# Router logits with tokens as the moving operand in two halves, row squares shared with VectorE, and expert rows scaled and turned in halves

## The chip, the cores and the metric

One Trainium2 chip, one core. The metric is the device time of one execution in microseconds (us), lower is better. All data are fp32 except a few one-hot tables in fp16.

## The reference, cut to what matters

One inference step of a hybrid decoder layer: 512 prompt tokens and 8 sample tokens, 520 in all, of width 2048. The part around the change is the end of the mixer and the hierarchical mixture of experts:

```python
x = x + mix @ w_out                       # 2048 x 2048
h = rmsnorm(x, g_ffn_norm)
lg = h @ w_rg + b_rg                      # 4 expert groups
le = h @ w_re + b_re                      # 8 experts in each: 36 router columns in all
grp = argmax(lg)                          # top 1 of 4 groups, then top 2 of 8 in it
out = sum over 2 chosen e of gate_e * (silu(h @ w_g[e]) * (h @ w_u[e])) @ w_d[e]
y = rmsnorm(x + out, g_final)
```

w_g and w_u of one expert are 2048 x 512, w_d is 512 x 2048. There are 32 experts, 12 MB of weights each.

## The kernel before, in words

Everything is in one SBUF arena of named regions and one PSUM tile of 8 banks (512 fp32 each). Each engine has one instruction stream written by hand; the order between engines is set by semaphores (`wait_ge`, `then_inc`), and a wait holds all that stands behind it in its stream.

**Output projection and router.** PE computes the 16 column tiles of `mix @ w_out` in turn (`outproj`, matmuls issued on L533: 128x128 weights, two halves of 260 tokens, 16 contraction steps). VectorE adds each to the residual (L1403), which gives `x2`, with features on partitions. After tiles 4, 8 and 12, and after the last, PE runs `rows_of_x2(g)` for the four tiles of group g (0 to 3). It turns the x2 columns into rows by PE transposes (L727), for five token tiles (four of 128, one of 8), through three rotating PSUM banks; ScalarE copies each turned tile to SBUF (L976), which frees the bank, and squares it with a row sum (L980). Then PE adds the group's share to the router logits (L732): the tokens are the stationary operand (128x128 loads), the 36 router columns the moving one, 5 token tiles x 4 contraction steps. So logits end with tokens on partitions, in bank 7. SyncE stores the rows of each group to a DRAM table `x2_rows` and loads weights in between.

**Routing.** After group 3, VectorE sums the squares (L1407), ScalarE takes the root (L982), VectorE inverts it, puts it beside the rows (L1415, L1416; SyncE then stores group 3, with the scale, and issues three of the first expert's weight chunks behind it), scales the logits (L1419), and runs a long chain of small operations: maxima, one-hots, ranks (PE, L768), places in blocks. Two one-hot tables (L1497, L1500) are multiplied on PE (L774) and give, for each block of up to 64 tokens (CAP) of one expert, the list of its tokens. Lists become indices (L1505 to L1509). GpSimd gathers a block's 64 rows from `x2_rows` by an indirect DMA (`gather`, L1117).

**Blocks.** A block is: ScalarE scales its rows (L994, 64x2048) into `xsc`; PE turns them (`turn_rows`, L787, 16 transposes in two groups of 8); VectorE evacuates the two groups (L1523) into `xtr`; PE multiplies gate and up weights (L807; outputs of two column halves go to PSUM partitions 0 to 63 and 64 to 127), turns the activation (L813), multiplies the down weights (L823); ScalarE evacuates (L1008), GpSimd scatters the rows (L1128). PE turns the rows of block n+1 between the up and the down product of block n. There are 34 blocks in this run: one for each expert, and two more. SyncE loads each weight chunk (six of 2 MB per expert) when PE has released the same chunk of the expert before (`s_fr`, L458, L461). The first expert's chunks are loaded without such a wait.

What the change touches: `rows_of_x2` and its ScalarE and VectorE partners (L971 to L980, L1400 to L1420), the lists product (L773, L1497), `scale_rows` (L989), `turn_rows` (L778), the first waits of the PE `expert` (L797) and the GpSimd stream before the first gather (L1133).

```python
            for b in range(20):                      # ScalarE
                g, i = b // 5, b % 5
                act.wait_ge(s_tr, b + 1)
                A(part, ps[0:n, 4 + b % 3, :], ACT.Copy).then_inc(s_trev, 1)
                ...
                A(rowjunk[0:n], part, ACT.Square, accum_out=row_part[0:n, i, g:g + 1]).then_inc(s_rss, 1)
```

## Time and profile before

| | before |
|---|---|
| median of 3 runs | 2068.12 us (2067.97 to 2071.73) |
| the profiled execution's own time | 2068.49 us |
| its span in the trace | 2066.7 us |
| PE busy | 1762.6 us (85%) |
| VectorE, ScalarE, GpSimd busy | 509.8, 325.3, 287.2 us |
| HBM read | 517.52 MB, 265 GB/s over the span |
| granted TensorE clock, mean | 0.944 of full speed |

The span is the stretch from the first to the last instruction of that execution; its own time is the span and 1.8 us around it. The profile names for each group of instructions its line, its engine, its shape and its mean length. The chain of waits follows the execution back from its end, at each step to what released it. The stages on the clock of the trace: projections, state space and attention until about 675 us, the output projection and its router groups until 926 us, routing until 956 us, the expert blocks until about 2001 us, the final sum and norm until the end. A fp32 matmul leaves two records in the trace, a transpose one.

### The profile page before, as it was taken

The page shows a single profiled execution, that of the slowest core. Times are in us where ns is not written, and L with a number is a line of the kernel's source. Part 1 is how long each engine was busy: PE and PEld are TensorE (multiplying, and loading weights), DVE is VectorE, ACT ScalarE, POOL GpSimd, SP SyncE. Part 2 cuts the span into 40 slices and gives each one's busy share as a digit, 9 for nine tenths or more (in the row PEclk, how much of TensorE's full clock was granted, in tenths as well). Part 3 has the DMA queues.
Part 4 walks back from the last instruction along what each step waited for, and adds up shares of the span by engine and source line. Part 5 has one row for each costly group of instructions (what it writes and reads, how often), then busy time and mean ns, then how long its engine had stood idle before and what let it go on. Part 6 is the DMA issues. An engine that isn't in the chain of part 4 may idle for free.

```text
span 2066.7 us, 27101 instructions
## 1 busy us (share of the span) xinstructions
PE 1762.6 (85%) x10986; PEld 1238.5 (60%) x10987; DVE 509.8 (25%) x1090; ACT 325.3 (16%) x573; POOL 287.2 (14%) x225
## 2 busy tenths in 40 slices
PE   7999999999899999985887787778787888977880
PEld 6888888887578888873544444434444454544440
DVE  6410999535365200014000000000000000000006
ACT  4003111004623011111111110101010111101112
POOL 0681322215800000000000000000000000000000
PEclk9999999999999999997999999998999999999895
DMA  5264121336954223317999999999999597999995
GB/s 234 64 153 111 68 81 61 122 147 190 14 199 162 102 82 125 140 37 292 386 405 422 395 413 395 406 391 393 393 398 393 199 399 324 412 403 411 414 416 218
DMA packets 88821, 535.86 MB, mean 259 GB/s; under 512 B 28761, under 2 KB 37465, under 8 KB 43673
## 3 DMA queue, kind: packets, MB, share of 16 engines
q1 hardware_dynamic: 74528, 513.81, 66.0%
q0 software_dynamic: 8800, 19.17, 3.2%
q10 hardware_dynamic: 5440, 2.13, 0.6%
q8 instruction: 39, 0.64, 0.1%
q14 instruction: 14, 0.11, 0.0%
HBM read 517.52 MB, written 30.91 MB: 265 GB/s over the span
## 4 chain that ended last, share of the span: by engine, by line
PE 53%; DMA 38%; POOL 3%; DVE 3%; ACT 2%; issue 1%; SPq 0%; POOLq 0%; ACTq 0%; DVEq 0%
DMA arena<-w_up_in 36%; PE psum L533 35%; PE psum L807 11%; PE psum L823 2%; DMA arena<-y_rows 1%; PE psum L662 1%; PE psum L668 1%; PE psum L570 1%; PE psum L787 1%; DVE arena L1564 1%; PE psum L732 1%; DVE arena L1557 1%; DMA y_rows<-arena 0%; POOL arena L1040 0%; POOL arena L1043 0%
## 5 line engine op out<-in xcount | busy, mean ns | idle before, releaser
L533 PE MATMUL psum<-arena 128*128 128x260 f32 x3328 | 741.5, 386 | 18.0 <-ACT arena L845 13.1
L533 PEld LDWEIGHTS psum<-arena 128*128 128x128 f32 x3328 | 637.1, 192 | 118.5 <-issue 10.2
L807 PE MATMUL psum<-arena 128*64 128x256 f32 x4352 | 541.8, 408 | 177.3 <-DMA arena<-w_up_in 150.5
L807 PEld LDWEIGHTS psum<-arena 128*64 128x64 f32 x4352 | 331.3, 148 | 397.0 <-DMA arena<-w_up_in 174.2
L823 PE MATMUL psum<-arena 128*64 128x512 f32 x1088 | 255.0, 623 | 16.9 <-ACT arena L1003 16.1
L1550 DVE TENSOR_TENSOR arena<-arena,psum 128x256 f32<-128x256 f32 x34 | 14.3, 421 | 959.9 <-PE psum L807 959.9
L823 PEld LDWEIGHTS psum<-arena 128*64 128x64 f32 x1088 | 78.1, 143 | 171.9 <-issue 143.5
L1128 POOL DMA_INDIRECT y_rows<-arena x34 | 33.9, 996 | 986.3 <-ACT arena L1008 941.2
L1003 ACT ACTIVATE arena<-psum 128x256 f32<-128x256 f32 x34 | 13.1, 384 | 509.2 <-PE psum L813 509.2
L787 PEld LDWEIGHTS psum<-arena 64*128 64x128 f32 x560 | 64.8, 203 | 22.1 <-issue 22.1
L1008 ACT ACTIVATE arena<-psum 128x512 f32<-128x512 f32 x68 | 36.9, 594 | 261.2 <-PE psum L823 261.2
L787 PE MATMUL psum<-arena 64*128 64x64 f32 x560 | 69.6, 276 | 8.8 <-ACT arena L994 8.8
L994 ACT ACTIVATE arena<-arena 64x2048 f32<-64x2048 f32 x35 | 69.8, 1995 | 19.7 <-DMA arena<-x_rows,arena 17.2
L1403 DVE TENSOR_TENSOR arena<-psum,arena 128x520 f32<-128x520 f32 x16 | 11.2, 700 | 223.4 <-PE psum L533 223.4
L1254 DVE TENSOR_TENSOR arena<-arena 128x64 f32<-128x64 f32 x128 | 45.3, 354 | 79.5 <-ACT arena L865 69.3
L1523 DVE TENSOR_TENSOR arena<-psum,arena 128x512 f32<-128x512 f32 x70 | 48.4, 692 | 29.8 <-PE psum L787 29.7
L883 ACT ACTIVATE arena<-psum 64x520 f32<-64x520 f32 x16 | 9.6, 601 | 263.9 <-PE psum L533 148.5
L1135 POOL MEMSET arena<- 128x4 f32 x2 | 0.1, 102 | 364.0 <-PE psum L732 364.0
L1259 DVE TENSOR_TENSOR arena<-arena 128x64 f32 x128 | 49.2, 385 | 4.4
L976 ACT ACTIVATE arena<-psum 128x512 f32<-128x512 f32 (+1 forms) x20 | 11.6, 581 | 225.4 <-PE psum L727 225.4
L1257 DVE TENSOR_TENSOR arena<-arena 128x64 f32<-128x64 f32 x128 | 46.4, 362 | 0.0
L1073 POOL TENSOR_TENSOR arena<-arena 128x520 f32<-128x520 f32 x16 | 20.8, 1300 | 170.5 <-ACT arena L885 131.8
(294 smaller groups left out, 1076.1 us busy)
## 6 DMA issues: line engine op xcount, KB each, us to landing
arena<-w_down_in SPq DMA_DIRECT2D x64, 2048.0 KB, 26.1
arena<-w_gate_in SPq DMA_DIRECT2D x64, 2048.0 KB, 28.1
arena<-w_up_in SPq DMA_DIRECT2D x64, 2048.0 KB, 27.7
arena<-w_in_in SPq DMA_DIRECT2D x32, 1024.0 KB, 4.8
arena<-w_out_in SPq DMA_DIRECT2D x16, 1024.0 KB, 4.8
arena<-k_cache_in SPq DMA_DIRECT2D x8, 1024.0 KB, 6.8
arena<-v_cache_in SPq DMA_DIRECT2D x8, 1024.0 KB, 4.8
arena<-y_rows SPq DMA_DIRECT2D x8, 1024.0 KB, 8.1
```

What stands on the lines that cost most here:

```text
L533: last = mm(pair(n)[:, h, :], w(kk), rhs(kk)[:, HALF * h:HALF * (h + 1)], start=(kk == begin), stop=(kk == kn - 1 and stop))
L787: last = pe.transpose(ps[:, 3 + g, CAP * m:CAP * (m + 1)], rows[:, 8 * g + m, :], ident[0:CAP, 0:CAP])
L807: last = mm(ps[64 * h:64 * h + 64, i // 2, 0:256], xtr[:, kk, :], w[:, kk, 256 * h:256 * (h + 1)], start=(kk == 0), stop=(kk == 15))
L823: last = mm(ps[64 * h:64 * h + 64, 5 + b, :], act_col[:, kk % 2, 64 * (kk // 2):64 * (kk // 2) + 64], wd[:, kk, 1024 * h + 512 * b:1024 * ...
L994: A(xsc[0:CAP], xrow[j][0:CAP, 0:DM], ACT.Copy, scale=xrow[j][0:CAP, DM:DM + 1]).then_inc(s_sc_x, 1)
L1008: A(yrow[:, 512 * b:512 * (b + 1)], ps[:, 5 + b, :], ACT.Copy).then_inc(s_yv, 1)
L1073: tt(rope_t[:, 0], rope_in[:, m % 2, 0], cosr, ALU.mult)
L1128: pool.indirect_dma_start(out=y_rows, out_offset=bass.IndirectOffsetOnAxis(ap=idx_now[:, 2 + j:3 + j], axis=0), in_=yrow, in_offset=None, ...
L1254: tt(scan_t[:, 0], column(it * 4 + s), lam_same, ALU.mult).then_inc(s_scan, 1)
L1257: tt(scan_t[:, 2], scan_t[:, 0], column(it * 4 + (s + 1)), ALU.add).then_inc(s_scan, 1)
L1259: tt(column(it * 4 + (s + 1)), scan_t[:, 2], scan_t[:, 1], ALU.add).then_inc(s_scan, 1)
L1523: tt(xtr[:, 8 * g:8 * g + 8, :], ps[:, 3 + g, :].rearrange("p (k n) -> p k n", n=CAP), gtab[:, 8 * g:8 * g + 8].unsqueeze(2).to_broadcast( ...
```

## The change

- In `rows_of_x2` the router weights (128x36) become the stationary operand and the tokens the moving one, in two parts of 256 and 264 tokens that go to PSUM partitions 0 to 35 and 64 to 99 of bank 7. This product stands after the first three token tiles are turned and before the last two. After group 3 the 36x520 logits are copied to SBUF in two parts (ScalarE the second, between its copies of tiles 2 and 3; VectorE the first, before its square of tile 3), and PE turns them into token rows in bank 0 (five small transposes).
- The squares of group 3 move from ScalarE to VectorE. The two constant tables upper16 and ones16 are now made after the row scales instead of before the wait for the row sums.
- The slot one-hots are 64 columns wide instead of 128; PE writes the lists twice, to partitions 0 to 63 and 64 to 127, in 20 matmuls instead of 10.
- GpSimd issues an indirect DMA whose 64 indices are all out of bounds, once the logits are in PSUM, and waits for its end before it goes on to the first gather.
- `scale_rows`, and the waits in `turn_rows` and `expert`, go by halves: ScalarE scales the eight k of half g (64x1024, in runs of 8 elements), PE turns that half as soon as it is scaled, and the first two gate chunks wait for one half each.

```diff
--- before.py
+++ after.py
@@ -225,7 +225,8 @@
         s_rss, s_rrt, s_rrs = sem("row_sumsq"), sem("row_root"), sem("row_rstd")
         s_hr = sem("h_row_ready")
         s_x2st = sem("x2_stored")
-        s_lg = sem("logits_psum")
+        s_lg, s_lgc, s_lgr = sem("logits_psum"), sem("logits_copied"), sem("logit_rows_psum")
+        s_warm = sem("idle_transfer_done")
         s_ra, s_rb = sem("router_act"), sem("router_dve")
         s_pos = sem("positions_psum")
         s_hot, s_lst = sem("one_hots_ready"), sem("lists_psum")
@@ -267,6 +268,8 @@
         iota_b, iota_s, valid, tok, half_of = col(NBLK), col(P), col(5), col(5), col(1)
         router_const = view(ro_at + 642, NBLK + P + 11)
         logit = col(180).rearrange("p (t n) -> p t n", t=5)
+        cut = 2 * P
+        logit_cols = [region("X", cut, 520), region("X", T - cut, 520 + cut)]
 
         keep = Cols(ms + 4 * XW + DM // 2)
         gate_w = keep(10).rearrange("p (t j) -> p t j", t=5)
@@ -278,13 +281,14 @@
         more_i = keep(1).bitcast(U32)
+        idle_i = keep(1).bitcast(U32)
 
         rt = Cols(ea + 2 * XW)
-        lo16 = rt(5 * P).bitcast(F16).rearrange("p (c s) -> p c s", c=10)
+        lo16 = rt(5 * CAP).bitcast(F16).rearrange("p (c s) -> p c s", c=10)
         hv16 = rt(10 * NBLK).bitcast(F16).rearrange("p (c v b) -> p c v b", c=10, v=2)
         in_group, elow, rest, elow2, rank = (rt(160).rearrange("p (t e) -> p t e", t=5) for _ in range(5))
         hot = rt(320).rearrange("p (c e) -> p c e", e=NE)
@@ -716,24 +720,36 @@
 
             def rows_of_x2(g):
 
-                pe.wait_ge(s_x2, 4 * g + 4)
-                if g == 0:
-                    pe.wait_ge(s_gwr, 1)
-                for i, n in enumerate(TOKS):
-                    b = 5 * g + i
+                def turned_tile(i):
+                    n, b = TOKS[i], 5 * g + i
                     if b >= 3:
                         pe.wait_ge(s_trev, b - 2)
                     for m in range(4):
                         last = pe.transpose(ps[0:n, 4 + b % 3, P * m:P * (m + 1)],
                                             x2[:, 4 * g + m, P * i:P * i + n], ident)
                     last.then_inc(s_tr, 1)
-                for i, n in enumerate(TOKS):
-                    for kk in range(4 * g, 4 * g + 4):
-                        last = mm(ps[0:n, 7, 36 * i:36 * (i + 1)], x2[:, kk, P * i:P * i + n], wr[:, kk, :],
-                                  start=(kk == 0 and i == 0), stop=(kk == 15), skip_group_check=True)
+
+                pe.wait_ge(s_x2, 4 * g + 4)
+                if g == 0:
+                    pe.wait_ge(s_gwr, 1)
+                for i in range(3):
+                    turned_tile(i)
+                for kk in range(4 * g, 4 * g + 4):
+                    for h in range(2):
+                        last = mm(ps[64 * h:64 * h + 36, 7, 0:(cut, T - cut)[h]], wr[:, kk, :],
+                                  x2[:, kk, cut * h:(cut, T)[h]], start=(kk == 0), stop=(kk == 15),
+                                  skip_group_check=True)
                 if g == 3:
                     last.then_inc(s_lg, 1)
-
+                for i in range(3, 5):
+                    turned_tile(i)
+                if g == 3:
+                    pe.wait_ge(s_lgc, 2)
+                    for i, n in enumerate(TOKS):
+                        c = P * i - (cut if i >= 2 else 0)
+                        last = pe.transpose(ps[0:n, 0, 36 * i:36 * (i + 1)], logit_cols[i >= 2][0:36, c:c + n],
+                                            ident[0:36, 0:36])
+                    last.then_inc(s_lgr, 1)
 
             def outproj(n, k0, kn, begin=0, stop=True):
                 for kk in range(k0, kn):
@@ -771,18 +787,19 @@
 
             pe.wait_ge(s_hot, 1)
             for c in range(10):
-                last = mm(ps[:, 4, 0:2 * NBLK].rearrange("p (v b) -> p v b", v=2), lo16[:, c, :], hv16[:, c],
-                          start=(c == 0), stop=(c == 9))
+                for h in range(2):
+                    last = mm(ps[64 * h:64 * h + 64, 4, 0:2 * NBLK].rearrange("p (v b) -> p v b", v=2), lo16[:, c, :],
+                              hv16[:, c], start=(c == 0), stop=(c == 9), skip_group_check=True)
             last.then_inc(s_lst, 1)
 
             def turn_rows(n):
 
-                pe.wait_ge(s_sc_x, n + 1)
-                if not first(n):
-                    pe.wait_ge(s_xte, n * 2)
-                pe.sem_inc(s_turn, 1)
                 rows = xsc[0:CAP, :].rearrange("p (m k) -> p k m", k=16)
                 for g in range(2):
+                    pe.wait_ge(s_sc_x, n * 2 + (g + 1))
+                    if not first(n):
+                        pe.wait_ge(s_xte, n * 2 + (g - 1))
+                    pe.sem_inc(s_turn, 1)
                     for m in range(8):
                         last = pe.transpose(ps[:, 3 + g, CAP * m:CAP * (m + 1)], rows[:, 8 * g + m, :],
                                             ident[0:CAP, 0:CAP])
@@ -794,9 +811,10 @@
                 else:
                     pe.wait_ge(s_tab, 1)
                     loaded = pe.value_load(loads_i[0:1, bass.ds(n, 1)], min_val=16, max_val=16 * NE)
-                pe.wait_ge(s_xte, n * 2 + 2)
                 for i in range(4):
                     w, c = (wg, wu)[i // 2], i % 2
+                    if i < 2:
+                        pe.wait_ge(s_xte, n * 2 + (i + 1))
                     pe.wait_ge(s_ld[i], loaded)
                     if i == 0 and not first(n):
                         pe.wait_ge(s_si, n)
@@ -974,6 +992,11 @@
                 part = x2_of[i][0:n, 512 * g:512 * (g + 1)]
                 act.wait_ge(s_tr, b + 1)
                 A(part, ps[0:n, 4 + b % 3, :], ACT.Copy).then_inc(s_trev, 1)
+                if b == 17:
+                    act.wait_ge(s_lg, 1)
+                    A(logit_cols[1][0:36], ps[64:100, 7, 0:T - cut], ACT.Copy).then_inc(s_lgc, 1)
+                if g == 3:
+                    continue
                 act.wait_ge(s_trev, b + 1)
                 if b:
                     act.wait_ge(s_rss, b)
@@ -989,9 +1012,11 @@
             def scale_rows(n, j, it):
 
                 act.wait_ge(s_gat[j], it * 16 + 16)
-                if not first(n):
-                    act.wait_ge(s_xt, n * 2)
-                A(xsc[0:CAP], xrow[j][0:CAP, 0:DM], ACT.Copy, scale=xrow[j][0:CAP, DM:DM + 1]).then_inc(s_sc_x, 1)
+                for g in range(2):
+                    if not first(n):
+                        act.wait_ge(s_xt, n * 2 + (g - 1))
+                    part = [r[0:CAP, 0:DM].rearrange("p (m k) -> p m k", k=16)[:, :, 8 * g:8 * g + 8] for r in (xsc, xrow[j])]
+                    A(part[0], part[1], ACT.Copy, scale=xrow[j][0:CAP, DM:DM + 1]).then_inc(s_sc_x, 1)
 
             def expert(n, j, it):
                 scale_rows(n + 1, 1 - j, it + j)
@@ -1120,7 +1145,7 @@
                     bounds_check=T - 1, oob_is_err=False).then_inc(s_gat[j], 16)
 
             def expert(n, j, it):
-                pool.wait_ge(s_sc_x, n + 1)
+                pool.wait_ge(s_sc_x, n * 2 + 2)
                 gather(n + 2, j)
                 pool.wait_ge(s_is, n + 1)
                 pool.wait_ge(s_yv, n * 2 + 2)
@@ -1133,7 +1158,12 @@
             pool.wait_ge(s_lg, 1)
             for j in range(2):
                 pool.memset(xrow[j][:, DM:XW], 0.0).then_inc(s_z0, 1)
-            pool.wait_ge(s_z0, 2)
+            pool.wait_ge(s_z0, 3)
+            pool.indirect_dma_start(
+                out=xrow[0][0:CAP, 0:DM // 2], out_offset=None, in_=t["w_glu"].rearrange("a p n -> (a p) n"),
+                in_offset=bass.IndirectOffsetOnAxis(ap=idle_i[0:CAP], axis=0),
+                bounds_check=T - 1, oob_is_err=False).then_inc(s_warm, 16)
+            pool.wait_ge(s_warm, 16)
             pool.wait_ge(s_x2st, 16 * 8)
             for j in range(2):
                 gather(j, j)
@@ -1398,12 +1428,20 @@
                 stt(z2[:, n], z2[:, n], gso[:, n:n + 1], rz, ALU.mult, ALU.mult).then_inc(s_mix, 1)
 
             dve.wait_ge(s_x2l, 16)
+            dve.memset(idle_i, int(BIG) - 1).then_inc(s_z0, 1)
             for n in range(16):
                 dve.wait_ge(s_op, n + 1)
                 tt(halves(x2[:, n]), pair(n), halves(x2[:, n]), ALU.add).then_inc(s_x2, 1)
-            dve.tensor_copy(upper16, region("upper", P))
-            dve.memset(ones16, 1.0)
-            dve.wait_ge(s_rss, 20)
+            for i, n in enumerate(TOKS):
+                dve.wait_ge(s_trev, 16 + i)
+                if i == 0:
+                    dve.wait_ge(s_rss, 15)
+                if i == 3:
+                    dve.wait_ge(s_lg, 1)
+                    dve.tensor_copy(logit_cols[0][0:36], ps[0:36, 7, 0:cut]).then_inc(s_lgc, 1)
+                part = x2_of[i][0:n, 1536:DM]
+                stt(rowjunk[0:n], part, 1.0, part, ALU.mult, ALU.mult, accum_out=row_part[0:n, i, 3:4]).then_inc(s_rss, 1)
+                dve.wait_ge(s_rss, 16 + i)
             dve.tensor_reduce(row_sum, row_part, X, ALU.add).then_inc(s_rrs, 1)
             link(dve.memset(logit, 0.0))
             dve.wait_ge(s_rrt, 1)
@@ -1414,9 +1452,11 @@
             dve.memset(x2_of[4][:, DM + 1:XW], 0.0)
             dve.tensor_copy(x2row[:, :, DM:DM + 1], row_rstd[:, 0:4].unsqueeze(2))
             dve.tensor_copy(x2_of[4][:, DM:DM + 1], row_rstd[:, 4:5]).then_inc(s_hr, 1)
-            dve.wait_ge(s_lg, 1)
+            dve.tensor_copy(upper16, region("upper", P))
+            dve.memset(ones16, 1.0)
+            dve.wait_ge(s_lgr, 1)
             for i, n in enumerate(TOKS):
-                last = stt(logit[0:n, i, :], ps[0:n, 7, 36 * i:36 * (i + 1)], row_rstd[0:n, i:i + 1], rbias[0:n],
+                last = stt(logit[0:n, i, :], ps[0:n, 0, 36 * i:36 * (i + 1)], row_rstd[0:n, i:i + 1], rbias[0:n],
                            ALU.mult, ALU.add)
             link(last)
 
@@ -1494,7 +1534,7 @@
             tt(o_, o_, b_, ALU.add)
             link(stt(w_, b_, -float(CAP), p_, ALU.mult, ALU.add))
             link(stt(by_choice(w_), by_choice(w_), 1.0, both(valid), ALU.add, ALU.mult))
-            tt(lo16, iota_s.unsqueeze(1).to_broadcast([P, 10, P]), over(w_, P), ALU.is_equal)
+            tt(lo16, iota_s[:, 0:CAP].unsqueeze(1).to_broadcast([P, 10, CAP]), over(w_, CAP), ALU.is_equal)
             link(tt(wide_b, iota_b.unsqueeze(1).to_broadcast([P, 10, NBLK]), over(o_, NBLK), ALU.is_equal))
             tt(hv16[:, :, 0, :], wide_b, over(id_, NBLK), ALU.mult)
             tt(hv16[:, :, 1, :], wide_b, over(tok1, NBLK), ALU.mult).then_inc(s_hot, 1)
```

## Rows read from the trace of the kernel before

**Rows 1.** The page, its chain that ended last, by engine.
```profile
PE 53%; DMA 38%; POOL 3%; DVE 3%; ACT 2%; issue 1%; SPq 0%; POOLq 0%; ACTq 0%; DVEq 0%
```

**Rows 2.** Windows: PE, PEld, DVE, ACT, POOL busy (instructions), PE clock, DMA share, GB/s.
```profile
900.00:918.00 18.00, 17.91 (x82) 15.20 (x80) 0.75 (x2) 0.00 (x0) 0.00 (x0) 1.00 0.00 1
...
1100.00:1300.00 200.00, 160.31 (x1086) 85.67 (x1082) 11.77 (x30) 22.72 (x31) 11.70 (x12) 0.92 1.01 406
...
1600.00:1650.00 50.00, 40.76 (x296) 22.23 (x294) 1.92 (x5) 7.08 (x9) 3.90 (x4) 0.97 0.54 203
```

**Rows 3.** Timeline of router group 1: start, length, what, [idle before <- releaser].
```profile
802.14 1.95 PE L727 MATMUL psum<-arena 128*128 128x128 f32 x16
...
802.77 0.60 ACT L976 ACTIVATE arena<-psum 128x512 f32<-128x512 f32 x1 [58.52 <-PE psum L727]
...
804.03 0.58 ACT L976 ACTIVATE arena<-psum 128x512 f32<-128x512 f32 x1
...
804.67 0.60 PE L727 MATMUL psum<-arena 128*8 128x128 f32 x4 [0.58 <-ACT arena L976]
...
805.10 4.03 PE L732 MATMUL psum<-arena 128*128 128x36 f32 x40
```

**Rows 4.** Chain of waits: the projection behind router group 1 (start, length, what).
```profile
809.13 57.99 PE psum L533 x256
```

**Rows 5.** Chain of waits in a stretch of blocks that wait for no weights.
```profile
1640.69 13.81 PE psum L807 x128
1654.50 1.92 PE psum L787 x16
```

**Rows 6.** Timeline of router group 3 and the row sums.
```profile
917.95 0.70 DVE L1403 TENSOR_TENSOR arena<-psum,arena 128x520 f32<-128x520 f32 x1 [13.33 <-PE psum L533]
918.57 0.22 DVE L1404 CAST arena<-arena 128x128 f16<-128x128 f32 x1
...
918.71 2.01 PE L727 MATMUL psum<-arena 128*128 128x128 f32 x16 [0.79 <-DVE arena L1403]
918.76 0.17 DVE L1405 MEMSET arena<- 128x128 f16 x1
919.40 0.60 ACT L976 ACTIVATE arena<-psum 128x512 f32<-128x512 f32 x1 [45.51 <-PE psum L727]
...
925.73 0.17 DVE L1407 TENSOR_REDUCE arena<-arena 128x5 f32<-128x20 f32 x1 [6.80 <-ACT arena L980]
```

**Rows 7.** Timeline of the one-hots and the lists product.
```profile
939.85 1.49 DVE L1497 TENSOR_TENSOR arena<-arena 128x1280 f16<-128x1280 f32 x1
...
941.94 0.66 DVE L1499 TENSOR_TENSOR arena<-arena 128x480 f16<-128x480 f32 x1
...
943.23 0.98 PE L774 MATMUL psum<-arena 128*128 128x96 f16 x10 [8.15 <-DVE arena L1500]
```

**Rows 8.** Timeline of the first two gathers.
```profile
946.10 1.88 POOL L1117 DMA_INDIRECT arena<-x_rows,arena  x1 [20.03 <-DVE arena L1509]
...
948.29 0.95 POOL L1117 DMA_INDIRECT arena<-x_rows,arena  x1 [0.31 <-issue]
```

**Rows 9.** Chain of waits at the first gather.
```profile
946.10 4.75 DMA arena<-x_rows,arena
```

**Rows 10.** Windows beside the first gather (columns as in rows 2).
```profile
942.00:946.00 4.00, 0.98 (x10) 0.77 (x10) 2.82 (x9) 0.00 (x0) 0.00 (x0) 0.50 1.01 430
946.00:950.00 4.00, 0.00 (x0) 0.00 (x0) 3.19 (x5) 0.00 (x0) 2.84 (x2) 0.50 0.66 248
```

**Rows 11.** Timeline of the first block until its first released weight chunk.
```profile
950.88 2.00 ACT L994 ACTIVATE arena<-arena 64x2048 f32<-64x2048 f32 x1 [17.17 <-DMA arena<-x_rows,arena]
...
953.02 2.00 PE L787 MATMUL psum<-arena 64*128 64x64 f32 x16 [8.82 <-ACT arena L994]
954.25 1.50 DVE L1523 TENSOR_TENSOR arena<-psum,arena 128x512 f32<-128x512 f32 x2 [5.00 <-PE psum L787]
...
955.81 15.89 PE L807 MATMUL psum<-arena 128*64 128x256 f32 x128 [0.78 <-DVE arena L1523]
...
961.55 3.78 SPq L458 DMA_DIRECT2D arena<-w_gate_in  x2
```

**Rows 12.** Window in which the first block's PE clock rises (columns as in rows 2).
```profile
958.00:960.00 2.00, 2.00 (x14) 1.19 (x12) 0.20 (x2) 0.42 (x1) 0.94 (x1) 0.60 0.00 0
```

**Rows 13.** DMA to landing of all gathers (the line L1117), least, median, most.
```profile
DMA to landing us min/median/max: 3.6/13.7/16.8
```

**Rows 14.** Timeline: a later row scaling, in a block that waits for no weights.
```profile
1641.77 2.00 ACT L994 ACTIVATE arena<-arena 64x2048 f32<-64x2048 f32 x1
```

## The prediction

> **What bounds the kernel now.** I read the chain of waits first: PE holds 53% of it and DMA 38% [rows 1]. Two stages share the span between them, so I went on to windows [rows 2]. In the output projection (900 to 918 us) PE is busy 17.91 of 18 us at clock 1.00 and the DMA engines are idle: PE sets the time there, and whatever PE does between two column tiles adds to it. In the blocks (1100 to 1300) the DMA share is 1.01 at 406 GB/s while PE is busy only 160 of 200 us: there the stream of expert weights sets the time. The exception is around the two extra blocks (1600 to 1650, DMA share 0.54), where an expert has a second block and its weights can't be released; there PE sets the time for two or three blocks. Between the two stages, from 918 to 956 us, one chain of small steps runs through all engines. Its end matters: the second expert's first weight chunk is issued at 961.55 us, when PE has used the first block's first chunk, which began after 955.81 [rows 11]. From there the stream is full, so what is saved before 955.81 should arrive at the end whole, and what is changed inside the blocks should hardly show.
>
> **Router groups 0 to 2.** Group 1 stands for three alike. PE starts to turn at 802.14 [rows 3] and is back in the projection at 809.13 [rows 4]: 6.99 us. In it, 40 logit records take 4.03 us, some 0.10 each: the 128x128 loads set this pace. The fifth tile starts only at 804.67, when ScalarE's second copy is done (804.03 + 0.58).
> The new logits are 4 steps x 2 parts = 8 matmuls, 16 records, of 256 or 264 columns. The nearest row is the gate and up product: fp32, 256 columns, outputs alternating between partitions 0 to 63 and 64 to 127, 128 records in 13.81 us, 0.108 each [rows 5]. The projection, with 260 columns over all partitions, takes 57.99 / 256 = 0.227 each [rows 4]. So in the first form two run beside one another. I take 0.108, because the new outputs lie in the same two halves: 16 x 0.108 = 1.7 us. The other end is 16 x 0.227 = 3.6.
> Turning: 16 transposes in 1.95 us [rows 3], with the last one's own length in it, are 0.11 each. The new group is 12 x 0.11 = 1.35, logits 1.7, then 8 x 0.11 = 0.9: 4.0 us, and some 0.2 where forms change. ScalarE's second copy is over 2.5 us after the start (804.61 - 802.14), before the fifth tile comes up at 1.35 + 1.7 + 0.45 = 3.5, so this wait is gone and nothing takes its place; ScalarE's copies and squares run on beside the projection, which hides them. Saved: 7.0 - 4.2 = 2.8 us each, **8.4 us** for three. SyncE's stores wait for the row copies, which are not later than before, but for the last two tiles by about 1 us under 58 us of cover [rows 4].
> On the change of form the trace speaks where gate and up end and the turning begins: 13.81 us of L807 from 1640.69, and L787 starts in the chain at 1654.50, with no piece between [rows 5]; over 128 records at 0.108 that leaves no more than about 0.2 us for it. A group changes form twice, so the bounds are 0 and 0.4 us, and the 0.2 above is their middle. The Trainium skill ("TensorEngine Tiling (Array Packing)", Key Properties) says that a change of tiling mode drains TensorE, which speaks against a tiled product put between transposes. By it the upper bound would hold each time, 1.2 us over the three groups where the sum has 0.6; no row shows more.
>
> **Group 3 to the row scales.** Before, ScalarE copies and squares five tiles from 919.40, and the sum starts at 925.73 [rows 6]. Now ScalarE only copies, 0.60 each: tiles 0 to 2 are over at 921.2. PE turns three tiles by 920.1 and has the logits at 922.0. ScalarE takes its part of them (about 0.4), then copies tile 3 until 923.1 and tile 4 until 923.7. VectorE's squares are over SBUF, 512 elements; nearest is its 128x520 addition, 0.70 us [rows 6]. Squares 0 to 2 end at 922.3; square 3 waits for tile 3 at 923.1, then the logit copy (0.35), then squares 3 and 4: the last ends at 924.9. What is late next is thus the copy of tile 3, behind ScalarE's wait for the logits. **0.8 us** earlier than 925.73. The five small transposes wait for both copies and are over at about 924.2, under the root and the reciprocal. The two constant tables, once under cover at 918.57 and 918.76 (0.22 and 0.17 [rows 6]), now stand between the row scales and the logits: **0.3 us** lost.
>
> **Lists.** The one-hots shrink from 1280 to 640 elements. 1.49 us for 1280 and 0.66 for 480 [rows 7] give 1.04 ns per element: **0.7 us** saved. The product goes from 10 to 20 matmuls of 96 columns; 10 took 0.98. If pairs overlap as above, nothing changes; if not, it costs up to 0.8 more. I take 0.1 lost.
>
> **First gather.** Its issue took 1.88 us, the next one's 0.95 [rows 8]. The out-of-bounds transfer takes the first-time share earlier, in the 20.03 us in which GpSimd idles [rows 8]. I take **0.9 us**, off the 4.75 us from the start of its issue to its landing [rows 9]; the ends are 0 (the extra belongs to this table or to real rows) and 1.2 (the issue gap ahead of it shrinks too). Against it: the gather starts about 2 us sooner, while the first expert's chunks, issued behind the row store and so only 0.8 us sooner, may still be landing; DMA is full until 946, and 66% busy for the next 4 us, gathers included [rows 10]. I charge 0.3 (0 to 1.5).
>
> **Halves.** From landing to the first gate matmul it was 950.88 to 955.81, 4.93 us [rows 11]: scaling 2.0, gap 0.14, turning 2.0, one evacuation 0.7. By halves: scaling 1.07 (0.60 for 512 elements [rows 6] and 2.00 for 2048 give 0.91 ns each), gap 0.15, turning 8 (1.0) while the other half is scaled, gap 0.1, turning 8 (1.0); the first evacuation lies under that, and the first gate chunk needs only this one. 3.3 us: **1.6 us** saved. The runs of 8 elements in ScalarE's pattern have no row; full speed is one end, and the length of the whole for each half (2.0) the other, by which landing to matmul is 2.0 + 2.0 + 0.15 + 1.0 = 5.15, 0.2 lost instead of 1.6 saved. I take full speed, as in both rows, which differ in source and in length and lie on one line. The half-speed clock (0.50, rising within 958 to 960 [rows 12]) then covers slightly more of the first matmuls: 0.2 lost.
>
> **Blocks.** Each turning now has two more waits and one more semaphore step. Under the weight stream that is free; in the two or three blocks that PE sets, and at the last, I charge 0.3 us in all. ScalarE's scaling ends at 1643.8 [rows 14] and its rows are turned at 1654.50 [rows 5]: 10.7 us of cover.
>
> **Sum.** 8.4 + 0.8 - 0.3 + 0.7 - 0.1 + 0.9 - 0.3 + 1.6 - 0.2 - 0.3 = 11.2 us. The profiled execution took 2068.49, 0.4 above the median of the three, 2068.12. 2068.49 - 11.2 = 2057.3; against the median 2056.9. I state 2057.0.
>
> **Rivals.**
> 1. The logit parts don't run beside one another. For: 36 columns are no form in the trace. Against: L807's 0.108. Each group loses 16 x 0.119 = 1.9; group 3's comes on the chain through ScalarE's wait: 4 x 1.9 = 7.6, so 2064.6. Chance 0.05.
> 2. The first gather meets the chunks and lands like the gathers under the full stream, 13.7 instead of 3.6 at best [rows 13]: about 9 us back, 2066. Against: at 946 DMA is already thinning [rows 10]. Chance 0.03.
> 3. Slower. The blocks are not paced by the DMA engines but by PE's releases, and the doubled waits, in each block's turning on PE, lengthen all 34 of them. It decides from 11.2 / 34 = 0.33 us per block; at 0.5 us it gives 2057 + 17 - 0.3 = 2074. Against: DMA share 1.01 [rows 2]. Chance 0.03.
> 4. The idle transfer brings nothing and ScalarE's runs of 8 are slow: 0.9 + 1.8 less, 2059.7. Chance 0.10.
> The forecast keeps 0.79.
>
> **How the numbers follow.** Low end: groups 3.1 each (+0.9), full gain of the gather (+0.6), no form change, 0.5; with 1 to 2 us of the weight stream's own variation 2053. High end: rival 4 with form changes at their upper bound (0.6), the lists product at its (0.7), half of the gather's (0.6) and a stream 1 us longer: 2062.6. The range is 2053 to 2063. 0.2% is 4.1 us, about what a measurement of this kernel can tell from no change: faster by more needs 2064.0 or less. The forecast and rival 4 are faster, 0.89, with a third of rival 1: 0.91. Same: the rest of rival 1 and rival 2, 0.06. Slower: 0.03.
>
> **What would show it.** From the first turning to the next projection record in groups 0 to 2: 4.2 us, not 7.0. The row sums 6.2 us after the addition's end, not 7.1. L1497 at 0.83 us. The first real gather's issue at 0.95. Landing to the first gate matmul 3.3. The first gate matmul of block 0 near 944.1 in place of 955.81 (the sum without the last two terms is 11.7), and 0.5 us more from there to the end of the span, within 2 us. If the last fails, the blocks were not paced as I say. A logit record pace of 0.2 us would prove rival 1, an L994 half of 2 us rival 4.

## The result, and the profile after

| | before | after |
|---|---|---|
| median of 8 executions | 2067.31 us | 2054.08 us |
| the profiled execution's own time | 2068.49 us | 2055.94 us |
| its span | 2066.7 us | 2054.1 us |
| ratio after to before | | 0.9928, 95% interval 0.9915 to 0.9941 |

One of the eight executions of the kernel after took 3459.05 us at a granted clock of 0.917 (0.944 to 0.953 in the other seven); it is left out of the ratio, and without it the median is 2053.97 us.

The change is faster by 0.72%, 14.9 us of 2067.3. The ratio puts the new time at 2052.4 us, just under the low end of the range (2053), and the gain at 14.9 us where 11.2 was forecast (12 to 18 us by the interval). By the medians the gain is 13.2 us and the time lies inside the range, and two later comparisons of the same kernels gave 0.9932 and 0.9937, 14.0 and 13.0 us. So the distance to the range is within the noise. The direction and the place were right; a term was missing.

First the router group. This is the chain of waits of the kernel after, from group 1 to group 2 (start, length, what); it answers to [rows 3, 4].

```profile
796.66 1.31 PE psum L728 x12
797.97 1.91 PE psum L739 x16
799.88 1.02 PE psum L728 x8
800.90 56.11 PE psum L537 x256
857.01 1.31 PE psum L728 x12
```

Twelve transposes, the new product, eight transposes: no ScalarE in the chain any more. But the row to look at is the fourth. The same 256 records of the projection, which the change does not touch, take 56.11 us instead of 57.99 [rows 4]. The windows behind the group say why. First the kernel before (PE, PEld, DVE, ACT, POOL busy, then PE clock, DMA share, GB/s), in rows that I had not read ahead of the prediction:

```profile
808.00:810.00 2.00, 2.00 (x18) 1.77 (x18) 0.00 (x0) 1.04 (x3) 0.00 (x0) 0.86 0.36 140
810.00:812.00 2.00, 2.00 (x6) 1.52 (x6) 0.00 (x0) 0.00 (x0) 0.00 (x0) 0.50 1.06 355
812.00:814.00 2.00, 2.00 (x9) 1.66 (x8) 0.00 (x0) 0.00 (x0) 0.00 (x0) 0.79 0.21 37
814.00:816.00 2.00, 2.00 (x11) 1.74 (x10) 0.00 (x0) 0.00 (x0) 0.00 (x0) 1.00 0.00 0
```

The same windows of the kernel after:

```profile
798.00:800.00 2.00, 2.00 (x18) 1.10 (x19) 0.00 (x0) 1.97 (x6) 0.00 (x0) 1.00 0.86 328
800.00:802.00 2.00, 2.00 (x14) 1.77 (x14) 0.00 (x0) 1.94 (x5) 0.00 (x0) 1.00 0.42 172
802.00:804.00 2.00, 2.00 (x10) 1.73 (x10) 0.00 (x0) 1.40 (x5) 0.00 (x0) 1.00 0.18 71
```

Before, the granted clock falls to 0.50 (1.2 GHz) just after the projection has resumed, with PE busy in all of these windows: 6 records in a 2 us window instead of 11. Window by window, some 3.4 us at half speed follow each of groups 0 to 2. After, there is no such stretch. From group 1 to group 2, first turning to first turning, it was 64.8 us and is 60.4: 2.6 from the group itself, 1.9 from the projection behind it. Of these 1.9 the clock is about 1.7, half of the 3.4 us at half speed; the experiments below measure it.

Then the stretch from the last addition to the first gate matmul. Timeline of the kernel after; it answers to [rows 6, 7, 8, 11]:

```profile
903.37 0.70 DVE L1434 TENSOR_TENSOR arena<-psum,arena 128x520 f32<-128x520 f32 x1 [13.33 <-PE psum L537]
...
908.19 1.06 ACT L994 ACTIVATE arena<-psum 128x512 f32<-128x512 f32 x2 [0.20 <-PE psum L728]
908.70 1.06 POOL L1162 DMA_INDIRECT arena<-w_glu_in,arena  x1 [0.93 <-POOL arena L1160]
908.87 0.42 DVE L1441 COPY arena<-psum 36x256 f32<-36x256 f32 x1 [1.25 <-ACT arena L994]
...
910.65 0.18 DVE L1445 TENSOR_REDUCE arena<-arena 128x5 f32<-128x20 f32 x1
...
925.03 0.83 DVE L1537 TENSOR_TENSOR arena<-arena 128x640 f16<-128x640 f32 x1
...
927.75 1.01 PE L791 MATMUL psum<-arena 128*64 128x96 f16 x20 [7.49 <-DVE arena L1540]
...
929.85 1.76 DVE L1552 TENSOR_TENSOR arena<-arena 128x1536 f32<-128x1536 f32 x1
930.58 1.86 POOL L1142 DMA_INDIRECT arena<-x_rows,arena  x1 [20.82 <-DVE arena L1549]
932.74 0.94 POOL L1142 DMA_INDIRECT arena<-x_rows,arena  x1 [0.30 <-issue]
...
936.71 2.19 ACT L1019 ACTIVATE arena<-arena 64x1024 f32<-64x1024 f32 x2 [17.81 <-DMA arena<-x_rows,arena]
938.00 2.16 PE L804 MATMUL psum<-arena 64*128 64x64 f32 x16 [9.24 <-ACT arena L1019]
...
940.09 16.11 PE L825 MATMUL psum<-arena 128*64 128x256 f32 x128
```

From the addition's start to the first gate matmul it was 37.86 us and is 36.72: 1.1 us saved (1.5 and 1.9 in two later traces of the kernel after, 36.32 and 35.93), where the terms of the prediction for this stretch come to 3.3. Its chain of waits holds the gather:

```profile
930.58 6.11 DMA arena<-x_rows,arena
```

The first real gather is as slow to issue behind the idle transfer (1.86 us) as without it (1.88 [rows 8]), and takes 6.11 us to land instead of 4.75 [rows 9].

### The profile page after: what moved, and what is told of

The parts are those of the page before. It is cut to its first block, busy times and chain, and to the rows that moved or that the text cites. A ratio compares the mean times of both kernels' runs of the same rounds, so it can differ in the third digit from the quotient of the medians.

```text
span 2054.1 us, 27081 instructions
## 1 busy us (share of the span) xinstructions
PE 1745.0 (85%) x10905; PEld 1233.7 (60%) x10906; DVE 512.2 (25%) x1102; ACT 328.6 (16%) x599; POOL 288.2 (14%) x226
## 4 chain that ended last, share of the span: by engine, by line
PE 52%; DMA 38%; POOL 3%; DVE 3%; issue 2%; ACT 1%; SPq 0%; POOLq 0%; DVEq 0%; ACTq 0%
DMA arena<-w_up_in 36%; PE psum L537 35%; PE psum L825 11%; PE psum L841 2%; DMA arena<-y_rows 1%; PE psum L666 1%; PE psum L672 1%; PE psum L574 1%; DVE arena L1604 1%; PE psum L804 1%; DVE arena L1597 1%; DMA y_rows<-arena 0%; POOL arena L1065 0%; POOL arena L1068 0%; DVE arena L1612 0%
## 5 line engine op out<-in xcount | busy, mean ns | idle before, releaser
L825 PEld LDWEIGHTS psum<-arena 128*64 128x64 f32 x4352 | 341.6, 147 | 392.7 <-DMA arena<-w_up_in 177.5
L841 PE MATMUL psum<-arena 128*64 128x512 f32 x1088 | 249.9, 612 | 18.0 <-ACT arena L1028 16.1
L841 PEld LDWEIGHTS psum<-arena 128*64 128x64 f32 x1088 | 77.2, 140 | 168.7 <-issue 139.2
L1019 ACT ACTIVATE arena<-arena 64x1024 f32<-64x1024 f32 x70 | 76.3, 1140 | 18.4 <-DMA arena<-x_rows,arena 17.8
L804 PEld LDWEIGHTS psum<-arena 64*128 64x128 f32 x560 | 64.8, 202 | 22.6 <-issue 22.5
L1434 DVE TENSOR_TENSOR arena<-psum,arena 128x520 f32<-128x520 f32 x16 | 11.2, 700 | 210.0 <-PE psum L537 210.0
```

The lines of the kernel that those rows point to most:

```text
L804: last = pe.transpose(ps[:, 3 + g, CAP * m:CAP * (m + 1)], rows[:, 8 * g + m, :], ident[0:CAP, 0:CAP])
L825: last = mm(ps[64 * h:64 * h + 64, i // 2, 0:256], xtr[:, kk, :], w[:, kk, 256 * h:256 * (h + 1)], start=(kk == 0), stop=(kk == 15))
L841: last = mm(ps[64 * h:64 * h + 64, 5 + b, :], act_col[:, kk % 2, 64 * (kk // 2):64 * (kk // 2) + 64], wd[:, kk, 1024 * h + 512 * b:1024 * ...
L1019: A(part[0], part[1], ACT.Copy, scale=xrow[j][0:CAP, DM:DM + 1]).then_inc(s_sc_x, 1)
```

## The experiments

Fourteen runs of twelve kernels, each beside the kernel before on the same chip. Seven of them (no idle transfer, late table, early chunks, whole rows, squares on ScalarE, k_tail3, m_best_noidle) are one profiled execution each: only their traces are read, not their times. "Issue" and "first gate matmul" are counted from the start of the last addition, since the profiled executions already differ by up to 5.7 us at their first router group (736.1 to 741.8 us), in stages that no edit touches.

**Old product, old place** (changed kernel otherwise):

```diff
-                for i in range(3):
+                for i in range(5):
                     turned_tile(i)
-                for kk in range(4 * g, 4 * g + 4):
-                    for h in range(2):
-                        last = mm(ps[64 * h:64 * h + 36, 7, 0:(cut, T - cut)[h]], wr[:, kk, :],
-                                  x2[:, kk, cut * h:(cut, T)[h]], ...)
+                for i, n in enumerate(TOKS):
+                    for kk in range(4 * g, 4 * g + 4):
+                        last = mm(ps[0:n, 7, 36 * i:36 * (i + 1)], x2[:, kk, P * i:P * i + n], wr[:, kk, :], ...)
-                for i in range(3, 5):
-                    turned_tile(i)
```

> The changed kernel with the router product of before (tokens stationary, 36 columns moving, after all five turned tiles); all else as changed. My theory: the router product accounts for nearly all of the gain. From the first turning of group 1 to that of group 2 it was 64.8 us before and 60.4 us changed, of which 2.6 us is the group itself and 1.9 us the projection behind it, where the granted clock fell to 0.50 for some 3 us before and stayed at 1.00 in the changed kernel. Expected: 64.8 us per period, the fall back in all three, and a time of 2066 to 2068 us, ratio to before 0.999. Rival: the projection behind the groups is quicker for another reason (queues, stores, the moved squares): then the period is 62.5 to 63 us, the clock stays at 1.00, and the ratio is 0.995 to 0.997.

Measured: ratio 0.9989 (0.9973 to 1.0004). The period is 64.8 us and the clock falls behind all three groups, 3.4 us each. Windows:

```profile
814.00:816.00 2.00, 2.00 (x6) 1.61 (x5) 0.00 (x0) 0.00 (x0) 0.00 (x0) 0.50 1.03 380
```

and the projection in its chain of waits:

```profile
813.56 57.99 PE psum L537 x256
```

So the router product is nearly the whole change in the time. The rival falls. One thing stands beside it: this kernel has its row sums 5.74 us after the last addition and its first gate matmul after 33.78, where the changed kernel needs 7.28 and 36.72. In group 3 the new product, in its new place, thus costs something of the 13.4 us that it saves in groups 0 to 2: 1.5 us by the time the first gather is issued (27.21 against 25.76), and 2.9 by the first gate matmul in these two traces (2.2 against the quickest of the changed kernel's three). Against the kernel before, whose figure is 37.86, the trace has 4.1 us less here, and the time shows 2.3 (0.8 more to 5.6 less): too few executions to say whether they arrive.

**Old product, new place**: the same old product, with `range(3)` ahead of it and `range(3, 5)` behind, so that PE waits for no copy.

> As the run before, but the old router product stands between the third and the fourth turned tile, so that PE waits for no copy. Theory 1, the old form itself (40 records of 36 moving columns) brings the clock down: the fall behind each group stays, the wait goes, period 64.2 us, ratio to before about 0.998. Theory 2, the wait of 0.6 us for the copy and the thin work around it bring it down: no fall, period 62.4 us, ratio about 0.995.

Measured: ratio 0.9986 (0.9963 to 1.0009). Its chain of waits, groups 0 and 1:

```profile
738.85 4.51 PE psum L739 x40
743.36 1.90 PE psum L728 x8
745.26 57.80 PE psum L537 x256
803.06 1.31 PE psum L728 x12
804.37 3.86 PE psum L739 x40
808.24 1.02 PE psum L728 x8
809.26 56.11 PE psum L537 x256
```

The fall comes inside group 0 (6.8 us at half speed by 1 us windows) and not behind groups 1 and 2. Here PE had no idle in the group before the clock fell:

```profile
741.00:743.00 2.00, 2.00 (x19) 1.93 (x19) 0.00 (x0) 0.81 (x3) 0.00 (x0) 0.68 0.31 127
```

Without the wait, then, the old form brought the clock down in one group of three. In groups 1 and 2, at clock 1.00, the eight transposes behind the old product took 1.02 us, as behind the new one. The period of group 1 is 62.3 us. The total gains nothing over the run before, because in group 3 the squares stand behind the old, longer product: row sums after 9.81 us instead of 5.74, first gate matmul after 37.91 instead of 33.78.

**New product, old place**: the changed kernel with `range(5)` ahead of its product and nothing behind, so that the wait stays.

> The changed kernel with its new router product moved behind all five turned tiles, so that the wait for the copy stays. Theory 1 (the form brings the clock down): no fall behind the groups, period 60.9 us, ratio to before 0.9935 to 0.994. Theory 2 (the wait does): the fall stays, period 62.8 us, ratio 0.996.

Measured: ratio 0.9946 (0.9931 to 0.9960). No fall behind any group, though PE waits 0.58 us for the copy as before. Timeline and windows:

```profile
803.62 0.60 PE L728 MATMUL psum<-arena 128*8 128x128 f32 x4 [0.58 <-ACT arena L994]
804.15 1.98 PE L741 MATMUL psum<-arena 128*36 128x256 f32 x16
```

```profile
806.00:808.00 2.00, 2.00 (x11) 1.72 (x10) 0.00 (x0) 1.94 (x6) 0.00 (x0) 1.00 0.00 0
808.00:810.00 2.00, 2.00 (x11) 1.74 (x10) 0.00 (x0) 0.02 (x1) 0.00 (x0) 1.00 0.88 339
```

The second window also answers a rival that the windows before suggest, the burst of DMA traffic beside the low clock (share 1.06): here is a burst of 0.88 behind the group, at clock 1.00. The projection, in the chain of waits:

```profile
806.12 56.30 PE psum L537 x256
```

This gives the price of the clock like for like, since in both kernels the product stands directly ahead of the projection: 57.99 - 56.30 = 1.7 us a group. The other 0.2 of the 1.9 goes with what stands ahead of the projection (56.11 behind transposes). The period is 61.2 us. The four kernels in one table:

| product | place | period of group 1 | groups 0 to 2 with a fall |
|---|---|---|---|
| old | old | 64.8 us | 3 of 3 |
| old | new | 62.3 us | 1 of 3 |
| new | old | 61.2 us | none |
| new | new | 60.4 us | none |

In these traces the fall came only with the old form: with the wait in 6 of 6 groups (the kernel before and the first experiment), without it in 1 of 3. With the new form it came in none, in 13 traces of three groups each: the projection behind groups 0 and 1 takes 56.11 us in twelve of them and 56.30 in this one. So the new form is enough to keep the clock up. That the wait makes the fall more likely rests on the three groups of one trace and is not shown beyond them. Nor is it shown which property of the old form does it: it has fewer moving columns (36 against 256), more records (40 against 16) and is longer (3.86 against 1.91 us), and these were not varied one by one. The Trainium skill ("TensorE: Matmul & The Clock Gate", A second HAM failure mode: psum-queue depth-cycling) says that short idles between groups of matmuls can bring the clock down and up again between its two levels. The trace agrees with that for the old form with its wait of 0.58 us; the same idle in front of the new form did nothing, and in group 0 of the old form in the new place the clock fell without any.

**No idle transfer:** the indirect DMA on w_glu and its wait are left out.

```diff
-            pool.indirect_dma_start(
-                out=xrow[0][0:CAP, 0:DM // 2], ...).then_inc(s_warm, 16)
-            pool.wait_ge(s_warm, 16)
```

> The changed kernel without the out-of-bounds transfer. Theory: the transfer brings nothing, since the first real gather's issue takes 1.86 us behind it as it took 1.88 without it; that length ends 0.8 to 0.9 us after VectorE's table comparison of 1536 elements ends, so it is the comparison that holds it. Expected: issue 1.8 to 1.9 us, gap from the index to the issue 0.9 to 1.0 us, first gate matmul within 0.2 us of the changed kernel's, counted from the last projection record. Rival (it pays a first-time cost): issue or gap longer by 0.5 us or more.

Measured, timeline:

```profile
931.74 1.88 POOL L1142 DMA_INDIRECT arena<-x_rows,arena  x1 [22.91 <-DVE arena L1544]
```

Issue 27.30 us after the addition (27.21 with the transfer), first gate matmul after 36.27 (35.93 to 36.72 in three traces of the changed kernel): the transfer is worth 0.1 us at the issue and nothing after it.

**Late table:** the comparison of 1536 elements and the four operations behind it, moved behind the first block's evacuations.

```diff
             link(ts(idx_s, no[:, 0, :], half_of, None, ALU.add))
-            link(tt(ahead, upto.unsqueeze(1).to_broadcast([P, NBLK, NE]),
-                    iota_b.unsqueeze(2).to_broadcast([P, NBLK, NE]), ALU.is_le))
-            ...
             dve.wait_ge(s_gt, 16)
             rows_turned(0)
+            link(tt(ahead, upto.unsqueeze(1).to_broadcast([P, NBLK, NE]),
+                    iota_b.unsqueeze(2).to_broadcast([P, NBLK, NE]), ALU.is_le))
+            ...
```

> The changed kernel with the five table operations (the 1536-element comparison first) moved from right behind the first index to behind the evacuation of the first block's turned rows. Theory: the comparison holds GpSimd's first gather, so its issue falls from 1.86 to 0.95 us; the landing comes up to 0.9 us sooner, less if the weight chunks still fill the DMA engines. Rival: the first gather is long of itself, and its issue stays at 1.8 to 1.9 us. In both the first gate matmul may not come later, and SyncE's first released chunk is not held by the table (it is over about 1 us before).

Measured, timeline:

```profile
933.33 0.95 POOL L1142 DMA_INDIRECT arena<-x_rows,arena  x1 [20.83 <-DVE arena L1549]
```

The issue is 0.95 us: it was VectorE's comparison, not a first use. In every trace with the comparison in its old place the gather's issue runs until 0.8 to 0.9 us after the comparison ends (929.85 + 1.76 = 931.61 against 932.44 in the kernel after). From the issue to the scaling of the rows it took 5.83 us, 0.3 less than in the first trace of the changed kernel and inside the spread of its three (5.34 to 6.13), so no gain at the landing is shown; the weight chunks still filled the DMA engines (share 0.92 in the first microsecond of the issue). The Trainium skill ("SBUF — State Buffer", Who interferes with whom) says that GpSimd and a VectorE operation with two SBUF inputs exclude each other when GpSimd reads SBUF; it infers that writing descriptors is not held by it. The exclusion agrees with this trace. The issue of this indirect DMA, with its indices in SBUF, was held.

**Early chunks:**

```diff
-            store_x2(3)
             sp.wait_ge(s_op, 16)
             ...
             for i in (0, 2, 3):
                 load_chunk(i, 0)
+            store_x2(3)
```

> The changed kernel with the first expert's three remaining chunks issued when the last projection is done, ahead of the last row store instead of behind it, some 8 us sooner. Theory: the 6.1 us from the first gather's issue to its landing hold 1.3 to 1.4 us in which the gather shares the DMA engines with these chunks. Expected: engines idle when the gather is issued, 4.7 us from issue to landing (1.86 of issue still in it), first gate matmul 1.4 us sooner, counted from the last projection record. Rival: the landing stays above 5.5 us with idle engines, and the length comes from the gather itself.

Measured: windows beside the gather, here

```profile
930.00:932.00 2.00, 0.76 (x20) 0.57 (x16) 1.09 (x7) 0.00 (x0) 0.00 (x0) 0.50 0.00 0
```

and in the kernel after

```profile
930.00:932.00 2.00, 0.00 (x0) 0.00 (x0) 1.97 (x2) 0.00 (x0) 1.42 (x1) 0.50 0.98 418
```

With idle engines, 4.55 us pass from the issue to the scaling (5.34 to 6.13 in the three traces of the kernel after), and the first gate matmul comes after 35.13 us instead of 35.93 to 36.72. With the chunks in flight the same stretch read 4.6 to 7.0 us in the other traces with a long issue, so its size is no constant, but nothing in flight gives its low end.

**Whole rows:** `scale_rows`, `turn_rows` and the waits of `expert` as in the kernel before.

```diff
-                for g in range(2):
-                    ...
-                    A(part[0], part[1], ACT.Copy, scale=xrow[j][0:CAP, DM:DM + 1]).then_inc(s_sc_x, 1)
+                A(xsc[0:CAP], xrow[j][0:CAP, 0:DM], ACT.Copy, scale=xrow[j][0:CAP, DM:DM + 1]).then_inc(s_sc_x, 1)
```

> The changed kernel with rows scaled and turned whole, as before. Theory: the halves gain only in the first block, 1.5 us from landing to the first gate matmul (4.93 against 3.45), and cost nothing in the blocks: the stretch of two blocks that wait for no weights keeps its 23.7 us per block within 0.1. Rival: the halves' added waits lengthen each such block by 0.2 us or more, so that it is shorter here than in the changed kernel.

Measured: from landing to the first gate matmul 4.94 us (3.38 with halves). In the blocks that wait for no weights one block follows another after 23.65 us, 23.67 before ([rows 5], to the next such row at 1664.36) and in the kernel after, whose chain of waits has

```profile
1628.88 13.81 PE psum L825 x128
...
1652.55 13.84 PE psum L825 x128
```

The halves are worth 1.6 us once and cost nothing.

**Squares on ScalarE:** the `continue` for group 3 and VectorE's five squares go.

```diff
-                if g == 3:
-                    continue
```

> The changed kernel with the squares of group 3 back on ScalarE, between its copies. Theory: ScalarE then does 5 copies, 5 squares (1.24 us a pair) and the logit copy (0.4), so the row sums stand 8.2 to 8.8 us after the last projection record instead of 7.3, and the split saves 1 to 1.5 us beside the new router product. Rival: the wait for the logits before tile 3 sets the end in either case, and the difference is under 0.4 us.

Measured: row sums after 8.19 us (7.28 with the split): the split saves 0.9 us beside the new product, just under the 1 to 1.5 that was expected.

**Another group 3, and all three together.** k_tail3 turns all five tiles first and puts both logit copies behind ScalarE's row copies; l_best adds the late table and the early chunks; m_best_noidle is l_best without the transfer.

```diff
+                early = 3 if g < 3 else 5
+                for i in range(early):
+                    turned_tile(i)
...
-                if b == 17:
+                if b == 19:
                     act.wait_ge(s_lg, 1)
+                    A(logit_cols[0][0:36], ps[0:36, 7, 0:cut], ACT.Copy).then_inc(s_lgc, 1)
                     A(logit_cols[1][0:36], ps[64:100, 7, 0:T - cut], ACT.Copy).then_inc(s_lgc, 1)
```

> The changed kernel with another group 3: all five tiles are turned first, then comes the new router product, ScalarE copies both parts of the logits behind its five row copies, VectorE only squares, and the two constant tables are made before the squares. Theory: in the changed kernel the squares of tiles 3 and 4 wait for ScalarE's copy of tile 3, which waits for the logits; without that the row sums stand 5.8 us after the start of the last addition (5.74 where the old product was left in place) instead of 7.28, and with the tables out of the chain the first gather is issued 25.3 to 25.6 us after it instead of 27.21. Up to 1.8 us reach the first gate matmul, less what the gather then shares with the weight chunks. Rival: the logits, which now come 1 us later, set the end, and the gather is issued no sooner than 26.7 us.

> The changed kernel with three edits together: group 3 as in k_tail3, the table operations late, the weight chunks early. Theory: they add up, 1.8 + 0.9 + 1.4 = 4.1 us or a little less: issue of the first gather 0.95 us, 3.7 us from issue to landing, first gate matmul 32.4 to 33.2 us after the start of the last addition instead of 36.72, and a time 3.5 to 4.5 us under the changed kernel's, ratio to before 0.9905 to 0.992. Rival: the blocks take it back, since their stream of weights then starts the same way but the sum of its waits is fixed; then the stretch from the first gate matmul to the end is over 1112 us and the ratio stays at 0.993.

> The changed kernel itself, beside the three others of this call. Every theory expects its time of the first comparison, ratio to before 0.9915 to 0.994, first gate matmul 36.7 us after the start of the last addition; its stretch from there to the end tells how far that stretch varies from run to run (1106 to 1114 us in the kernels so far, with no order in them).

> As l_best, without the out-of-bounds transfer. Theory: the transfer brings nothing even when nothing else holds the gather: issue 0.95 us, and the gather is issued within 0.1 us of l_best's, counted from the last addition. Rival: its worth was hidden behind the comparison of 1536 elements, and here the first issue is 0.5 us or more longer.

| | row sums | issue | length of issue | issue to scaling | first gate matmul | from there to the end |
|---|---|---|---|---|---|---|
| after | 7.28 | 27.21 | 1.86 | 6.13 | 36.72 | 1114.0 |
| after_again | 7.28 | 27.21 | 1.86 | 5.73 | 36.32 | 1115.3 |
| after_3 | 7.29 | 27.21 | 1.85 | 5.34 | 35.93 | 1110.2 |
| k_tail3 | 5.74 | 25.61 | 1.85 | 5.02 | 34.01 | 1110.1 |
| l_best | 5.75 | 25.61 | 0.95 | 3.70 | 32.69 | 1110.1 |
| l_best_2 | 5.74 | 25.59 | 0.95 | 3.76 | 32.73 | 1112.1 |
| m_best_noidle | 5.74 | 25.70 | 1.06 | 3.80 | 32.88 | 1109.7 |

The timeline of l_best at its first gather:

```profile
933.88 0.95 POOL L1143 DMA_INDIRECT arena<-x_rows,arena  x1 [18.32 <-DVE arena L1547]
```

In the traces nearly all went as expected: 4.0 us less to the first gate matmul than in the first trace of the changed kernel (3.2 to 4.0 over its three), and the idle transfer worth 0.1 us. In k_tail3 the 2.7 us are more than the 1.8 expected, since the stretch from the issue to the scaling also came out shorter. In the times it did not: l_best 0.9938 (0.9918 to 0.9957), the changed kernel beside it 0.9932 (0.9914 to 0.9951). So both ran once more:

> The kernel of l_best again. It reaches the first gate matmul 4.0 us sooner than the changed kernel and releases the first gate chunk 3.5 us sooner, and yet its six times did not lie lower (medians 2052.65 and 2051.22). Theory: the gain passes through the blocks, whose length varies by several us from run to run, and eleven or twelve runs of each show 2 to 4 us. Rival: the stream of weights takes a gain at its start back, and the two kernels' means stay within 1 us.

> The changed kernel beside l_best_2. Theory: its mean over all runs of the two calls lies 2 to 4 us above that of l_best. Rival: within 1 us.

Measured: 0.9932 (0.9919 to 0.9946) and 0.9937 (0.9924 to 0.9951). Over all executions but the one of 3459 us, the changed kernel's mean is 2053.1 us (18 executions, standard deviation 3.0), l_best's 2053.0 (11, 2.1). The difference of the means is uncertain by about 1.9 us: a gain of 4 us would stand out of this, one of 2 only just, and none is there. It isn't shown where it went. The blocks did not lengthen in the traces: from the first gate matmul to the end l_best took 1110.1 and 1112.1 us, the changed kernel 1114.0, 1115.3 and 1110.2. What did differ lies ahead of every edit: the last addition started at 908.3 and 907.4 us in l_best's two traces, at 903.4, 906.8 and 904.0 in the changed kernel's (907.2 in k_tail3, 906.4 in m_best_noidle). That could be chance in so few executions, or a slower early stage in the edited program; it was not tried further. l_best is thus no better version by its time.

## Why the prediction was right or wrong

**Which stages set the time:** right for the projection. 3 x 4.5 us are saved in the router groups and 1.5 to 2.9 of them are lost again behind group 3, which leaves 10.5 to 11.9 us for the router product; putting back only the old one takes the ratio from 0.9928 to 0.9937 (three comparisons) to 0.9989, 10.7 to 12.6 us. For the blocks see the last item.

**Groups 0 to 2, the group itself:** right within 0.2 us each. The product of 16 records takes 1.91 us, forecast 1.7; the two parts do run beside one another (rival 1 falls). From the first turning to the next projection record it is 4.4 us instead of 7.0, forecast 4.2. The eight transposes behind it take 1.02 us instead of the 0.9 of the forecast, but they take 1.02 behind the old product too, so this is no cost of the change of form. A projection directly behind the new product takes 56.30 us instead of 56.11 behind transposes; the change of form can be at most these 0.2 us, and this is not separated from other causes.

**Groups 0 to 2, what follows them:** this step failed. The 2.8 us a group held nothing for the projection behind it, as if its 256 records took the same time in both kernels; they took 57.99 us before and 56.11 after, because the granted clock fell to 0.50 behind the old group and not behind the new one. I priced a projection record at 57.99 / 256 = 0.227 us and used it only as the other end for the new product. My own window at 900 to 918 has 82 such records in 17.91 us, 0.218 each, at clock 1.00 [rows 2]; I did not compare the two, and read no clock right behind a group. The missing term is 3 x 1.88 = 5.6 us, 3 x 1.7 = 5.1 of it clock, the largest single error.

**Group 3 to the row scales:** forecast 0.8, measured 0.5 (7.78 to 7.28). The late step was named rightly, the copy of tile 3 behind the logits. VectorE's squares take 0.74 us each with the row sum, and the logit copy comes 0.3 us later than drawn. The constant tables cost 0.27 (forecast 0.3).

**Lists:** 0.66 saved on the one-hots (forecast 0.7); the product took 1.03 instead of 0.99, so its pairs overlap too.

**First gather:** this step failed as well. The 0.9 us of first use don't exist; that length was the comparison on VectorE, which runs beside the first gather in both kernels. The stretch from the issue to the scaling, which holds the sharing with the weight chunks, took 0.6 to 1.4 us more than before (4.78 against 5.34 to 6.13) where I charged 0.3. Together +0.6 was forecast and -0.6 to -1.4 measured. Rival 4 thus held in its first half (the idle transfer brings nothing) and not in its second.

**Halves:** 4.93 to 3.38 us, 1.55 (forecast 1.6); ScalarE's runs of 8 go at full speed, 2.19 us for both halves against 2.14 drawn. First gate matmul to first released chunk went from 5.74 to 5.95 us, as the 0.2 charged for the clock.

**Blocks:** no cost to be seen where 0.3 was charged; the 23.67 us of a block that PE sets did not move, so the slower rival falls too.

**The sum:** 3 x (2.6 + 1.9) + 1.1 = 14.6 us against 14.9 by the ratio, and 13.0 and 14.0 in the later comparisons. The forecast's 11.2 lacked the 5.6 behind the groups and held some 2.2 too much in the tail; the two errors offset one another in part, and that the time came out so near the range is luck. The range took its ends from the terms I had and so missed by 0.6 us, less than three comparisons of the same two kernels differ by.

**That what is saved before the first gate matmul arrives whole:** the times agree with it for the router groups, not for the tail: the 4.0 us of l_best did not arrive. The prediction named a sign for it, 0.5 us more from the first gate matmul to the end of the span, within 2 us. It was 1110.9 us before and 1114.0, 1115.3 and 1110.2 after: 3.1 and 4.4 more and 0.7 less. Two of three fail the sign. But this stretch reads 1106.6 to 1115.3 us over all sixteen traces, so one trace could not decide it, and how the blocks are paced beyond the stretch that PE sets stays open.

## What to carry to other kernels

Where an engine's stage alternates between a dense product and a short, thin one, read the granted clock in the windows right behind the thin one, and compare the time of one unchanged record with that of the same record far from it; the price of the thin one includes what it does to the next. Before paying for a warm-up, look at what runs on the neighbour engine beside the slow first use. And when stages that no edit touches vary by several us, a gain of that size in a trace is not yet a gain in time.

## What the runs showed of the hardware that was not expected

- TensorE went down to 0.50 of its clock while PE was busy: 40 fp32 records of 36 moving columns behind 128x128 loads, with one wait of 0.58 us 4 to 5 us before the fall, did it behind 6 of 6 groups in two traces; without the wait in 1 of 3; 16 records of 256 columns with the wait, in none of 3.
- A comparison of 128x1536 elements on VectorE, with both inputs in SBUF, stretched the issue of an indirect DMA on GpSimd from 0.95 to 1.86 us.
- The same early stages, with the same instructions, reached the first router group between 736.1 and 741.8 us.
